# Two chained transformer blocks in fp32: another order of loads, splits and down products in the second block's feed-forwards, and two edits in the first feed-forward

## The chip, the cores and the metric

One core of a Trainium2 chip runs the whole program. The metric is the device time of one execution in microseconds, the median of three runs: 1930.71 us before the change (1929.75 to 1932.2). A difference of 0.2% is 3.9 us.

## What is computed

256 tokens of width 1024 go through a first block of two layers (feed-forward, mixer, feed-forward, each with a layer norm) and a second one of two layers (mixer, feed-forward, gated side input). Cut to what the change touches:

```python
def _swiglu(x, w1, w3, w2):                    # block 1, D_FF = 2816, four times
    return (jax.nn.silu(x @ w1) * (x @ w3)) @ w2

for i in range(DEPTH):                         # block 2, D_FF_2 = 4096, twice
    ...
    u = jax.nn.relu(rms_norm(h, ff_norm[i]) @ w_ff1[i])
    h = h + (u * u) @ w_ff2[i]
```

All of it is fp32 and must be as exact as fp32.

## The kernel before, in words

**Splitting.** TensorE multiplies in a rounded fp32 form. Each matrix is therefore split in a high part (a rounding copy by ScalarE) and a low part (the original less the high part, by VectorE), and a product is three matmuls: high by high, high by low, low by high. A weight unit has 128x2048 values. SyncE loads it into one of four slots of `raw`, ScalarE writes `whi` (for the trace `w_high`), VectorE writes `wlo` (`w_low`), and TensorE uses both in 12 matmuls of 512 columns for one half of the tokens, 24 for both. The slots form a ring. ScalarE may write a slot's high part only when TensorE has used what stood there before, which it learns from the semaphore `unit_used` (helper `used(name)`).

**Pairs (a Strassen-like form with seven products).** Most of the hidden width is computed in groups of four quarter matrices R11, R21, R12, R22 of the weights, loaded into `buf_v`, `buf_q`, `buf_u` and `buf_val`. Seven block products of 12 matmuls give what eight would: `b11`, `b21`, `v`, `x`, `w`, `y`, `b22`. Their weight operands are R11, R21, sums that VectorE forms in place in `buf_v` (`add_to`, one after another: R11+R12 for `v`, then +R22 for `x`, then +R21 for `y`), and R12+R22 in `buf_u` for `w`, which GpSimd makes by a DMA that adds (`w_sum`). The token operands are quarters of x and four sums of them (`form`). Results gather in four banks of `aux` (PSUM); ScalarE copies bank 1 out three times between products (`term1`, `term2`, `term3`) and a last time through the activation (`silu1`); VectorE combines them. The hidden values are then transposed on TensorE (`quad_T(q, 0)`, `quad_T(q, 1)`), split to `yT_high` and `yT_low`, and multiplied by the down weights (`down`, 24 matmuls, one unit of `w_ff2`).

**Block 2's feed-forward** (`ffn2`, `FFN2_ORDER`, `FFN2_DONE`) has two plain groups `h0`, `h1` (transposed by `plain_T(0)` and `plain_T(1)` into banks 2 and 3), whose down units are `d0_0`, `d0_1`, `d1_0`, `d1_1`, and three pairs q = 0, 1, 2, with down units `e0_0` to `e2_3`. Down units fill the time between the block products: pair 0 gets those of the plain groups, pair q those of pair q-1. On TensorE the order before is `d0_0`, `d0_1`, `plain_T(1)`, then for pair 0 `b11 b21 v x (d1_0 first half) w (d1_0 second half) y b22 (d1_1 first half) quad_T(0,0) (d1_1 second half) quad_T(0,1)`.

Product `v` writes bank 3 and must wait till that bank has been read after both `plain_T`, by VectorE's `plain_low_T(1)`:

```python
pe.wait_ge(aux_read[3], aux0[3] + PLAIN2 + q + 1)
block_product(ffn2_unit(i, f"v_{q}"), 3, *form(f, 0), True)
```

**What sets the order.** Each engine has its own list of instructions, written out by hand, and takes them strictly in that order; semaphores hold it where it must wait. SyncE's list of loads is `ffn2` and `quad_load2` there; R11 of the next pair is loaded when `y`'s low part has been made from the same buffer.

**Block 1's feed-forward** (`ffn1`) has the same parts with one down unit and other fills. In the very first one (l = 0, which = 0) GpSimd first adds the negated high part of `b21` to its low part by a DMA (`sums_by_dma`), and then makes `w`'s sum for pair 0 by the second DMA.

Of the kernel before, what the change touches and what calls it, by code (L numbers as in the profile page):

```python
# [121 lines left out]
def ffn2_units():  # L122

    order = ["h0_0", "h0_1", "h1_0", "h1_1", "d0_0", "d0_1",
             "b11_0", "b21_0", "v_0", "x_0", "d1_0", "w_0", "y_0", "b22_0", "d1_1"]
    done = ["h0_0", "h1_0", "d0_0", "d0_1",
            "b11_0", "b21_0", "v_0", "x_0", "w_0", "d1_0", "y_0", "b22_0", "d1_1"]
    for q in range(1, QUADS2):
        e = [f"e{q - 1}_{k}" for k in range(4)]
        order += [f"b11_{q}", f"b21_{q}", f"v_{q}", f"x_{q}", e[0], f"w_{q}", e[1], f"y_{q}", e[2], f"b22_{q}", e[3]]  # L130
        done += [f"b11_{q}", f"b21_{q}", f"v_{q}", f"x_{q}", e[0], f"w_{q}", e[1], f"y_{q}", e[2], f"b22_{q}", e[3]]
# [139 lines left out]
def build(nc, a, out, stop=None):  # L271
    ctx = ExitStack()
    with ctx:
# [100 lines left out]
        w_sum = sem("w_sum")  # L374
        b21_neg = sem("b21_neg")
# [169 lines left out]
        def _(sp):  # L545
# [154 lines left out]
            def ffn2(i):  # L700
# [43 lines left out]
        def _(pool):  # L744
# [42 lines left out]
            def sums_by_dma(l, which):  # L787
# [7 lines left out]
                for q in range(QUADS):  # L795
# [108 lines left out]
        def _(pe):  # L904
# [105 lines left out]
            def ffn2(i, tile1, before_last):  # L1010
# [89 lines left out]
                down("d0_1")  # L1100
                plain_T(1)
                for q in range(QUADS2):
# [22 lines left out]
                    if q > 0:  # L1125
                        down(fill[2])
                    pe.wait_ge(quad_read, combined + 2)
                    block_product(ffn2_unit(i, f"b22_{q}"), 3, *form(f, 3), False)
                    late = "d1_1" if q == 0 else fill[3]
                    down_part(late, 0)  # L1130
                    quad_T(q, 0)
                    down_part(late, 1).then_inc(unit_used, 1)
# [818 lines left out]
        def _(act):  # L1951
# [38 lines left out]
            def ffn2(i, tile1, before_last):  # L1990
# [69 lines left out]
                used("d0_1")  # L2060
                summed(0, 2)
                high_sum("x", 0, R11)
                for q in range(QUADS2):
# [7 lines left out]
                    high_plain("d1_0" if q == 0 else fill[0])  # L2071
                    used(f"b21_{q}")
                    act.wait_ge(w_sum, 16 * quads2_before(i, q) + 16)
                    high_sum("w", q, R12)
                    if q > 0:
                        used(f"v_{q}")
                        high_plain(fill[1])
                    used(f"x_{q}")
                    nc.scalar.copy(term2, aux[:, 1, :]).then_inc(quad_act, 1)
                    summed(q, 3)  # L2080
                    high_sum("y", q, R11)
                    if q > 0:
                        used(fill[0])
                        high_plain(fill[2])
# [4 lines left out]
                    used("d1_0" if q == 0 else fill[1])  # L2089
                    high_plain("d1_1" if q == 0 else fill[3])  # L2090
                    used(f"y_{q}")
                    nc.scalar.activation(silu1, aux[:, 1, :], ACT.Relu).then_inc(quad_act, 1)
                    if q + 1 < QUADS2:
                        loaded(q + 1, R11)
                        high_sum("b11", q + 1, R11)
                        if q > 0:
                            used(fill[2])
                        loaded(q + 1, R21)
                        high_sum("b21", q + 1, R21)
# [3 lines left out]
                        quad_high_T(q, 0)  # L2103
                        quad_high_T(q, 1)
                        used("d1_1" if q == 0 else fill[3])
                        summed(q + 1, 2)
# [1740 lines left out]
```

## Time and profile before

| | before |
|---|---|
| median of 3 runs | 1930.71 us (1929.75 to 1932.2) |
| the profiled execution | 1929.22 us, span 1927.4 us, mean clock share 0.996 |
| TensorE matmul busy | 1881.1 us (98%) |
| VectorE busy | 1494.9 us (78%) |
| ScalarE busy | 1050.0 us (54%) |
| GpSimd busy | 118.9 us (6%) |
| HBM read | 351.39 MB, 183 GB/s over the span |

The profiled execution's time is 1.8 us longer than its span. Matmuls overlap: one of 512 columns is shown with 389 ns, but the next begins 227 ns after it. In a row of the timeline the first number is the start, the second the time to the last end of the row; instructions of VectorE and ScalarE overlap their successor by 0.1 us, so that the starts, not the ends, tell the pace.

### The profile page before, as it was taken

Reading aid. Unit: us, or ns where it says so; the run is one execution under the profiler, and the core shown is the slowest. Engines: PE = TensorE matmul, PEld = TensorE weight load, DVE = VectorE, ACT = ScalarE, POOL = GpSimd, SP = SyncE. Lnnn points to the kernel's source line nnn. Section 1 sums busy time; section 2 is a strip of 40 time slices with the busy share of each in tenths; the row PEclk is TensorE's granted clock in tenths of the full one; section 3 lists DMA queues with packets and bytes.
Section 4 is the critical chain, followed back from the end, with each engine's and each line's share of the span. In section 5 each row is a group of like instructions: output and inputs, shape, how many; then the busy total and the mean of one; then the engine's idle time right before and its main releaser. Section 6 shows DMA issues by size and latency. Waiting matters only on the chain.

```text
span 1927.4 us, 22719 instructions
## 1 busy us (share of the span) xinstructions
PE 1881.1 (98%) x8944; PEld 1538.9 (80%) x8944; DVE 1494.9 (78%) x1663; ACT 1050.0 (54%) x1239; POOL 118.9 (6%) x186
## 2 busy tenths in 40 slices
PE   8999999999999999999999999999999999999999
PEld 7788788887888788878888788787778887777787
DVE  6887766778887888777667888778798766779975
ACT  6555444555555555543564655567655555655553
POOL 2001100001000000110000000011000000100000
PEclk9999999999999999999999999999999999999999
DMA  9865554348764766564445766444385545338651
GB/s 337 266 218 168 203 191 173 141 167 284 240 218 152 241 220 222 185 239 174 142 164 185 252 219 220 151 162 157 130 299 177 197 161 178 121 116 309 181 205 57
DMA packets 179177, 376.99 MB, mean 196 GB/s; under 512 B 7568, under 2 KB 51520, under 8 KB 176256
## 3 DMA queue, kind: packets, MB, share of 16 engines
q1 hardware_dynamic: 170512, 334.85, 49.1%
q0 software_dynamic: 8560, 40.69, 8.7%
q8 instruction: 72, 1.18, 0.2%
q14 instruction: 33, 0.27, 0.0%
HBM read 351.39 MB, written 1.05 MB: 183 GB/s over the span
## 4 chain that ended last, share of the span: by engine, by line
PE 80%; DVE 11%; DMA 3%; ACT 3%; DVEq 1%; issue 1%; SPq 0%; ACTq 0%; POOLq 0%
PE acc L926 49%; PE aux L996 15%; PE aux L926 10%; DVE w_low L2710 3%; DVE w_low L2835 2%; PE aux L941 1%; DMA buf_v<-w_ff 1%; DMA w_raw<-ffn_w 1%; DVE buf_v L2840 1%; PE aux L1364 1%; DVEq L2762 1%; DVE xT_low L2716 1%; DMA buf_u<-buf_val 1%; DMA w_low<-buf_q 1%; PE aux L1211 1%
## 5 line engine op out<-in xcount | busy, mean ns | idle before, releaser
L2710 DVE TENSOR_TENSOR w_low<-w_raw,w_high 128x2048 fp32r<-128x2048 f32 (+1 forms) x246 | 554.1, 2265 | 116.4 <-ACT w_high L1959 113.3
L1959 ACT CAST w_high<-w_raw 128x2048 fp32r<-128x2048 f32 (+1 forms) x246 | 462.2, 1895 | 177.4 <-PE acc L926 155.0
L926 PE MATMUL acc<-w_high,yT_high 128*128 128x512 f32 (+1 forms) x836 | 331.6, 397 | 2.5 <-DVE yT_low L2974 2.0
L926 PE MATMUL acc<-w_high,yT_low 128*128 128x512 f32 (+1 forms) x836 | 325.6, 389 | 0.0
L926 PE MATMUL acc<-w_low,yT_high 128*128 128x512 f32 (+1 forms) x836 | 324.9, 389 | 0.0
L926 PE MATMUL acc<-w_high,xT_high 128*128 128x512 f32 (+2 forms) x752 | 297.9, 396 | 6.9 <-DVE xT_low L2716 4.1
L926 PE MATMUL acc<-w_high,xT_low 128*128 128x512 f32 (+2 forms) x752 | 291.3, 387 | 0.0
L926 PE MATMUL acc<-w_low,xT_high 128*128 128x512 f32 (+2 forms) x752 | 290.9, 387 | 0.0
L926 PEld LDWEIGHTS acc<-w_high,yT_high 128*128 128x128 f32 x836 | 157.0, 188 | 38.2 <-issue 6.6
L926 PEld LDWEIGHTS acc<-w_high,yT_low 128*128 128x128 f32 x836 | 156.9, 188 | 33.0
L926 PEld LDWEIGHTS acc<-w_low,yT_high 128*128 128x128 f32 x836 | 157.2, 188 | 30.0
L926 PEld LDWEIGHTS acc<-w_high,xT_high 128*128 128x128 f32 x752 | 141.6, 188 | 41.4 <-DVE xT_low L2716 5.2
L926 PEld LDWEIGHTS acc<-w_high,xT_low 128*128 128x128 f32 x752 | 141.4, 188 | 28.9
L926 PEld LDWEIGHTS acc<-w_low,xT_high 128*128 128x128 f32 x752 | 141.7, 188 | 26.1
L2141 ACT CAST w_high<-buf_v 128x2048 fp32r<-128x2048 f32 x48 | 91.8, 1913 | 124.8 <-DVE buf_v L2964 81.8
L926 PE MATMUL aux<-w_high,xT_high 128*128 128x512 f32 x384 | 153.6, 400 | 2.6 <-DVE w_low L2710 1.6
L2959 DVE TENSOR_TENSOR w_low<-buf_v,w_high 128x2048 fp32r<-128x2048 f32 x48 | 109.9, 2290 | 52.4 <-ACT w_high L2141 52.4
L926 PE MATMUL aux<-w_high,xT_low 128*128 128x512 f32 x384 | 150.0, 391 | 0.0
L926 PE MATMUL aux<-w_low,xT_high 128*128 128x512 f32 x384 | 149.6, 390 | 0.0
L996 PE MATMUL aux<-w_high,form_high 128*128 128x512 f32 x288 | 113.7, 395 | 7.8 <-DVE w_low L2959 3.9
L996 PE MATMUL aux<-w_low,form_high 128*128 128x512 f32 x288 | 112.6, 391 | 0.0
L996 PE MATMUL aux<-w_high,form_low 128*128 128x512 f32 x288 | 112.6, 391 | 0.0
(411 smaller groups left out, 2754.5 us busy)
## 6 DMA issues: line engine op xcount, KB each, us to landing
w_raw<-w_in SPq DMA_DIRECT2D x52, 1024.0 KB
w_raw<-ffn_w SPq DMA_DIRECT2D x44, 1024.0 KB
w_raw<-w_ff SPq DMA_DIRECT2D x40, 1024.0 KB
w_raw<-ffn_w SPq DMA_DIRECT2D x78, 512.0 KB
buf_u<-buf_val POOLq DMA_DIRECT2D x18, 1024.0 KB, 7.0
w_raw<-w_branch SPq DMA_DIRECT2D x16, 1024.0 KB
buf_q<-ffn_w SPq DMA_DIRECT2D x12, 1024.0 KB, 6.6
buf_v<-ffn_w SPq DMA_DIRECT2D x12, 1024.0 KB, 8.5
```

Source lines behind the costliest of these rows:

```text
L926: last = nc.tensor.matmul(dst, lhs[:, kt, tok], rhs(j), start=(kt == k_first and q == 0), stop=(kt == k_last and q == 2))
L941: last = nc.tensor.transpose(aux[:, b, k * P:(k + 1) * P], src[:, t, kt * P:(kt + 1) * P], ident[:])
L996: last = nc.tensor.matmul(aux[:, b, :], lhs(k), rhs[:, s, k * NC:(k + 1) * NC], start=(first and k == 0 and m == 0), stop=(k == 3 and m == 2),
L1211: last = nc.tensor.transpose(aux[:, b, (2 * f + t) * P:(2 * f + t + 1) * P], h[:, f0:f0 + P], ident[:])
L1364: last = nc.tensor.transpose(aux[0:width, b, (2 * k + t) * P:(2 * k + t + 1) * P], src(t, h), ident[:])
L1959: nc.scalar.copy(whi[:, s, 0:size], raw[:, s, 0:size]).then_inc(slot_hi[s], 1)
L2141: nc.scalar.copy(whi[:, s, :], sum_raw[r]).then_inc(slot_hi[s], 1)
L2710: V.tensor_tensor(wlo[:, s, 0:size], raw[:, s, 0:size], cast(whi[:, s, 0:size]), ALU.subtract)\
L2716: V.tensor_tensor(dst_l[:, k, tok], src, cast(dst_h[:, k, tok]), ALU.subtract)\
L2762: dve.drain()
L2835: V.tensor_tensor(wlo[:, s, :], sum_raw[r], cast(whi[:, s, :]), ALU.subtract)\
L2959: V.tensor_tensor(wlo[:, s, :], sum_raw[r], cast(whi[:, s, :]), ALU.subtract)\
```

## The change

Block 2's feed-forwards, all three pairs of both:

- TensorE: `d0_1` moves from ahead of `plain_T(1)` to behind `v` of pair 0. The four down units of each pair now stand behind `v`, `x`, `w` and (the last) around the transposes: for pair 0 `v d0_1 x d1_0 w (d1_1 first half) y b22 quad_T(0,0) (d1_1 second half) quad_T(0,1)`, for q > 0 `v e0 x e1 w e2 y b22 quad_T(q,0) e3 quad_T(q,1)`.
- Slots: in pair 0 `w` takes the ring place before `x`, which is the slot that `d0_1` leaves.
- VectorE: `d0_1`'s low part goes behind `v`'s, `x`'s low part ahead of `plain_low_T(1)`; `w`'s ahead of the sum for `y` in pair 0; `d1_1`'s ahead of `y`'s; `b11` of the next pair ahead of the product that makes `silu1`'s operand.
- ScalarE: the high parts in the same manner; `w`'s now waits for `d0_1`'s use, and `b11` of pair 1 stands ahead of the activation `silu1`.
- SyncE: `d1_1` and `e0_1` are loaded earlier, `e0_0` later.

First feed-forward of block 1 alone: `activate(1, 0)` and the high and low parts of the first y stand ahead of `b11`'s, and `w`'s sum for pair 0 is made by VectorE behind `x`'s low part (semaphore `w_first`); GpSimd's adding DMA for that pair falls away, and the counts of `w_sum` move by one.

The core of the diff (left out: the tail of the last pair, the semaphore's declaration, the branch for q > 0 where it repeats):

```diff
@@ ffn2_units
     order = ["h0_0", "h0_1", "h1_0", "h1_1", "d0_0", "d0_1",
-             "b11_0", "b21_0", "v_0", "x_0", "d1_0", "w_0", "y_0", "b22_0", "d1_1"]
+             "b11_0", "b21_0", "v_0", "w_0", "x_0", "d1_0", "y_0", "b22_0", "d1_1"]
@@ sync, ffn2
-                for name in ("d1_0", "e0_0", "e0_1", "d1_1"):
+                for name in ("d1_0", "d1_1", "e0_1"):
                     load_ffn2(i, name)
-                for r in (R21, R12, R11, R22):
+                for r in (R21, R12, R11):
                     quad_load2(i, 1, r)
+                load_ffn2(i, "e0_0")
+                quad_load2(i, 1, R22)
@@ gpsimd, sums_by_dma
-                for q in range(QUADS):
+                for q in range(1 if l == 0 and which == 0 else 0, QUADS):
@@ tensor, ffn2
                 down("d0_0")
-                down("d0_1")
                 plain_T(1)
...
                     block_product(ffn2_unit(i, f"v_{q}"), 3, *form(f, 0), True)
+                    down("d0_1" if q == 0 else fill[0])
                     pe.wait_ge(quad_act, terms + 1)
                     block_product(ffn2_unit(i, f"x_{q}"), 1, *form(f, 2), False)
-                    if q == 0:
-                        down_part("d1_0", 0)
-                    else:
-                        down(fill[0])
+                    down("d1_0" if q == 0 else fill[1])
                     pe.wait_ge(quad_act, terms + 2)
                     block_product(ffn2_unit(i, f"w_{q}"), 1, *form(f, 1), False)
+                    late = "d1_1" if q == 0 else fill[3]
                     if q == 0:
-                        down_part("d1_0", 1).then_inc(unit_used, 1)
+                        down_part(late, 0)
                     else:
-                        down(fill[1])
+                        down(fill[2])
@@ scalar, ffn2
-                used("d0_1")
+                used("b11_0")
                 summed(0, 2)
                 high_sum("x", 0, R11)
@@ scalar, ffn1
+                first = l == 0 and which == 0
+                if first:
+                    activate(1, 0)
+                    plain_high_T(0)
                 used("h1_0")
                 loaded(0, R11)
                 high_sum("b11", 0, R11)
@@ vector, ffn2
                 multiply(1, 1)
-                low_plain("d0_1")
                 add_to(0, R11, R12)
                 low_sum("b21", 0, R21)
+                form_low(f, 0)
                 low_sum("v", 0, R11)
+                low_plain("d0_1")
                 add_to(0, R11, R22)
-                for n in range(FORMS):
+                for n in range(1, FORMS):
                     form_low(f, n)
+                low_sum("x", 0, R11)
                 plain_low_T(1)
@@ vector, ffn1
                     low_sum("x", q, R11)
+                    if first and q == 0:
+                        dve.wait_ge(r_full[R22], 16)
+                        V.tensor_tensor(sum_raw[R12], sum_raw[R12], sum_raw[R22], ALU.add).then_inc(w_first, 1)
                     low_plain(f"d{o - 3}")
                     add_to(q, R11, R21)
```

How the lists stand, with the semaphores each row waits on. VectorE in block 2's first feed-forward, from `b11`'s low part (the first row) to `plain_low_T(1)` (the last), before:

```order
L2835 TENSOR_TENSOR w_low<-buf_v,w_high 128x2048 [waits slot_hi0]
L2844 TENSOR_TENSOR buf_k<-buf_k,aux 128x512 [waits act_done]
L2710 TENSOR_TENSOR w_low<-w_raw,w_high 128x2048 [waits slot_hi3]
L2840 TENSOR_TENSOR buf_v<-buf_v,buf_u 128x2048 [waits r_full2]
L2835 TENSOR_TENSOR w_low<-buf_q,w_high 128x2048 [waits slot_hi1]
L2835 TENSOR_TENSOR w_low<-buf_v,w_high 128x2048 [waits slot_hi2]
L2840 TENSOR_TENSOR buf_v<-buf_v,buf_val 128x2048 [waits r_full3]
L2819 TENSOR_TENSOR form_low<-mix_param,form_high 128x512 [waits form_hi] x4
L2850 TENSOR_TENSOR yT_low<-aux,yT_high 128x512 [waits t_hi] x2
```

and the same stretch now:

```order
L2857 TENSOR_TENSOR w_low<-buf_v,w_high 128x2048 [waits slot_hi0]
L2866 TENSOR_TENSOR buf_k<-buf_k,aux 128x512 [waits act_done]
L2862 TENSOR_TENSOR buf_v<-buf_v,buf_u 128x2048 [waits r_full2]
L2857 TENSOR_TENSOR w_low<-buf_q,w_high 128x2048 [waits slot_hi1]
L2841 TENSOR_TENSOR form_low<-mix_param,form_high 128x512 [waits form_hi]
L2857 TENSOR_TENSOR w_low<-buf_v,w_high 128x2048 [waits slot_hi2]
L2732 TENSOR_TENSOR w_low<-w_raw,w_high 128x2048 [waits slot_hi3]
L2862 TENSOR_TENSOR buf_v<-buf_v,buf_val 128x2048 [waits r_full3]
L2841 TENSOR_TENSOR form_low<-mix_param,form_high 128x512 [waits form_hi] x3
L2857 TENSOR_TENSOR w_low<-buf_v,w_high 128x2048 [waits slot_hi0]
L2872 TENSOR_TENSOR yT_low<-aux,yT_high 128x512 [waits t_hi] x2
```

`d0_1`'s low part (from `w_raw`) moved behind `v`'s, and `x`'s low part, which stood behind `plain_low_T(1)`, now stands ahead of it.

ScalarE in pair 0 of the same feed-forward, from the copy `term1` on, before (`w` is the row from `buf_u`, `silu1` the ACTIVATE, and the row behind it `b11` of pair 1):

```order
L2070 COPY mix_param<-aux 128x512 [waits unit_used,form_lo]
L1959 CAST w_high<-w_raw 128x2048 [waits slot_full0]
L2005 CAST w_high<-buf_u 128x2048 [waits w_sum,unit_used]
L2079 COPY mix_param<-aux 128x512 [waits unit_used]
L2005 CAST w_high<-buf_v 128x2048 [waits sum_done]
L2086 COPY mix_param<-aux 128x512 [waits unit_used]
L2005 CAST w_high<-buf_val 128x2048 [waits r_full3]
L1959 CAST w_high<-w_raw 128x2048 [waits slot_full0,unit_used]
L2092 ACTIVATE mix_param<-aux 128x512 [waits unit_used]
L2005 CAST w_high<-buf_v 128x2048 [waits r_full0]
```

and now:

```order
L2069 COPY mix_param<-aux 128x512 [waits unit_used,form_lo]
L1958 CAST w_high<-w_raw 128x2048 [waits slot_full1,unit_used]
L2004 CAST w_high<-buf_u 128x2048 [waits w_sum,unit_used]
L2087 COPY mix_param<-aux 128x512 [waits unit_used]
L1958 CAST w_high<-w_raw 128x2048 [waits slot_full0]
L2004 CAST w_high<-buf_v 128x2048 [waits sum_done]
L2096 COPY mix_param<-aux 128x512 [waits unit_used]
L2004 CAST w_high<-buf_val 128x2048 [waits r_full3]
L2004 CAST w_high<-buf_v 128x2048 [waits r_full0,unit_used]
L2109 ACTIVATE mix_param<-aux 128x512 [waits unit_used]
```

`b11` of pair 1 (from `buf_v`, waiting on its load `r_full0`) moved ahead of the activation; the `unit_used` of `w` is now that of `d0_1`.

VectorE in the first feed-forward of block 1, from `x`'s low part to `w`'s, before and then now:

```order
L2959 TENSOR_TENSOR w_low<-buf_v,w_high 128x2048 [waits slot_hi1]
L2710 TENSOR_TENSOR w_low<-w_raw,w_high 128x2048 [waits slot_hi0]
L2964 TENSOR_TENSOR buf_v<-buf_v,buf_q 128x2048 [waits r_full1]
L2959 TENSOR_TENSOR w_low<-buf_u,w_high 128x2048 [waits slot_hi3]
...
L2999 TENSOR_TENSOR w_low<-buf_v,w_high 128x2048 [waits slot_hi1]
L3074 TENSOR_TENSOR buf_u<-buf_u,buf_val 128x2048 [waits r_full3]
L2732 TENSOR_TENSOR w_low<-w_raw,w_high 128x2048 [waits slot_hi0]
L3004 TENSOR_TENSOR buf_v<-buf_v,buf_q 128x2048 [waits r_full1]
L2999 TENSOR_TENSOR w_low<-buf_u,w_high 128x2048 [waits slot_hi3]
```

One more addition of a whole unit stands between `x`'s low part and that of the down unit `d1`.

## Rows read from the trace of the kernel before

**Rows 1.** The page: span, and busy time of TensorE and VectorE (share, instructions).

```profile
span 1927.4 us, 22719 instructions
PE 1881.1 (98%) x8944; PEld 1538.9 (80%) x8944; DVE 1494.9 (78%) x1663; ACT 1050.0 (54%) x1239; POOL 118.9 (6%) x186
```

**Rows 2.** Waits of TensorE: who waited for whom, us in total, times, longest.

```profile
PE aux L1058 <- DVE mix_param L2863: 4.7, 2, 3.0
...
PE aux L996 <- DVE w_low L2959: 3.9, 1, 3.9
PE aux L996 <- DVE yT_low L2850: 3.5, 4, 1.7
...
PE acc L926 <- DVE yT_low L2974: 2.0, 1, 2.0
```

**Rows 3.** Chain of waits in order of time (start, us, what): TensorE's paces.

```profile
60.38 4.51 PE aux L996 x12
...
1448.42 13.24 PE aux L996 x48
1461.66 5.44 PE acc L926 x24
...
1786.03 11.18 PE aux L996 x48
```

**Rows 4.** Busy time by stretch: us, engines' busy time, granted clock (PEclk), DMA share, GB/s.

```profile
60.40:63.50 3.10, 3.10 (x7) 2.44 (x8) 3.10 (x2) 1.59 (x1) 0.00 (x0) 0.50 0.68 198
1445.60:1452.70 7.10, 5.89 (x18) 4.63 (x19) 6.76 (x6) 2.62 (x3) 0.00 (x0) 0.53 0.45 92
1783.20:1789.00 5.80, 4.06 (x21) 3.33 (x22) 5.80 (x5) 1.21 (x3) 0.00 (x0) 1.00 0.63 132
```

**Rows 5.** Timeline of block 2's first feed-forward, TensorE: start of `d0_0`, `v`, `quad_T(0,1)`.

```profile
1398.32 0.39 PE L926 MATMUL acc<-w_high,yT_high 128*128 128x512 f32 x1
...
1416.19 0.50 PE L996 MATMUL aux<-w_high,form_high 128*128 128x512 f32 x1 [0.30 <-DVE yT_low L2850]
...
1445.62 1.60 PE L1058 MATMUL aux<-ident,mix_param 128*128 128x128 f32 x8 [3.03 <-DVE mix_param L2863]
```

**Rows 6.** Timeline, VectorE: `b11` low, forms, `plain_low_T(1)`; last, layer 2's `b11` low.

```profile
1398.62 2.29 DVE L2835 TENSOR_TENSOR w_low<-buf_v,w_high 128x2048 fp32r<-128x2048 f32 x1 [1.39 <-ACT w_high L2005]
1400.83 0.68 DVE L2844 TENSOR_TENSOR buf_k<-buf_k,aux 128x512 f32<-128x512 f32 x1
...
1412.43 2.50 DVE L2819 TENSOR_TENSOR form_low<-mix_param,form_high 128x512 fp32r<-128x512 f32 x4
1414.84 1.29 DVE L2850 TENSOR_TENSOR yT_low<-aux,yT_high 128x512 fp32r<-128x512 f32 x2
...
1737.61 2.29 DVE L2835 TENSOR_TENSOR w_low<-buf_v,w_high 128x2048 fp32r<-128x2048 f32 x1 [1.34 <-ACT w_high L2005]
```

**Rows 7.** Timeline, ScalarE: pair 1's `b11` high part, behind its load.

```profile
1435.59 1.91 ACT L2005 CAST w_high<-buf_v 128x2048 fp32r<-128x2048 f32 x1 [1.43 <-DMA buf_v<-w_ff]
```

**Rows 8.** Chain of waits, the loads of R11: pair 0, then pair 1.

```profile
1391.09 5.51 DMA buf_v<-w_ff
...
1427.76 7.81 DMA buf_v<-w_ff
```

**Rows 9.** Timeline of the first feed-forward, VectorE: low parts of `b11`, `x`, `d1`, `w`.

```profile
33.56 2.29 DVE L2959 TENSOR_TENSOR w_low<-buf_v,w_high 128x2048 fp32r<-128x2048 f32 x1 [2.07 <-ACT w_high L2141]
...
47.44 2.29 DVE L2959 TENSOR_TENSOR w_low<-buf_v,w_high 128x2048 fp32r<-128x2048 f32 x1 [0.18 <-ACT w_high L2141]
50.31 2.29 DVE L2710 TENSOR_TENSOR w_low<-w_raw,w_high 128x2048 fp32r<-128x2048 f32 x1 [0.58 <-ACT w_high L1959]
...
57.94 2.29 DVE L2959 TENSOR_TENSOR w_low<-buf_u,w_high 128x2048 fp32r<-128x2048 f32 x1 [3.13 <-ACT w_high L2141]
```

**Rows 10.** Chain of waits there: GpSimd's two adding DMAs.

```profile
32.04 11.18 DMA w_low<-buf_q
...
43.88 12.05 DMA buf_u<-buf_val
```

More of the change, by code:

```diff
@@ L2088, in ffn2 @@
                     high_sum("b22", q, R22)
[L2089 to L2092, printed above, removed]
                     if q + 1 < QUADS2:
-                        loaded(q + 1, R11)
-                        high_sum("b11", q + 1, R11)
-                        if q > 0:
-                            used(fill[2])
-                        loaded(q + 1, R21)
-                        high_sum("b21", q + 1, R21)
+                        if q == 0:
+                            used("d1_0")
+                            loaded(1, R11)
+                            high_sum("b11", 1, R11)
+                        else:
+                            used(fill[2])
+                            loaded(q + 1, R21)
+                            high_sum("b21", q + 1, R21)
+                        used(f"y_{q}")
+                        nc.scalar.activation(silu1, aux[:, 1, :], ACT.Relu).then_inc(quad_act, 1)
+                        if q == 0:
+                            loaded(1, R21)
+                            high_sum("b21", 1, R21)
+                        else:
+                            loaded(q + 1, R11)
+                            high_sum("b11", q + 1, R11)
+                        quad_high_T(q, 0)
                         used(f"b22_{q}")
@@ L2102, in ffn2 @@
                         high_sum("v", q + 1, R11)
[L2103 removed]
                         quad_high_T(q, 1)
[L2105 to L2107 removed]
                     else:
                         tail = [f"e{q}_{k}" for k in range(4)]
+                        used(f"y_{q}")
+                        nc.scalar.activation(silu1, aux[:, 1, :], ACT.Relu).then_inc(quad_act, 1)
                         high_plain(tail[0])
[L2111 removed]
+                        quad_high_T(q, 0)
                         high_plain(tail[1])
@@ L2186, in ffn1 @@
                 high_sum("b11", 0, R11)
-                activate(1, 0)
-                plain_high_T(0)
+                if not first:
+                    activate(1, 0)
+                    plain_high_T(0)
                 for n in range(FORMS):
@@ L2909, in ffn2 @@
                     V.tensor_tensor(term1, aux[:, 0, :], term1, ALU.add).then_inc(quad_read, 1)
+                    low_plain("d1_1" if q == 0 else fill[2])
                     low_sum("y", q, R11)
@@ L2920, in ffn2 @@
-                    V.tensor_tensor(silu1, silu1, aux[:, 1, :], ALU.mult).then_inc(h_ready, 1)
                     if q + 1 < QUADS2:
-                        low_sum("b11", q + 1, R11)
-                        add_to(q + 1, R11, R12)
-                        low_sum("b21", q + 1, R21)
+                        if q == 0:
+                            low_sum("b11", 1, R11)
+                        else:
+                            low_sum("b21", q + 1, R21)
+                        dve.wait_ge(quad_act, terms + 4)
@@ new lines, in ffn2 @@
+                        V.tensor_tensor(silu1, silu1, aux[:, 1, :], ALU.mult).then_inc(h_ready, 1)
+                        if q == 0:
+                            add_to(1, R11, R12)
+                        dve.wait_ge(unit_used, ffn2_done(i, f"b22_{q}"))
+                        V.tensor_tensor(term2, aux[:, 3, :], term2, ALU.subtract).then_inc(quad_read, 1)
+                        squared_relu(term2, combined + 3)
+                        if q > 0:
+                            low_sum("b11", q + 1, R11)
+                            add_to(q + 1, R11, R12)
@@ L2925, in ffn2 @@
+                        quad_low_T(q, 0)
+                        if q == 0:
+                            low_sum("b21", 1, R21)
+                        low_sum("v", q + 1, R11)
+                        quad_low_T(q, 1)
+                        add_to(q + 1, R11, R22)
                     else:
                         tail = [f"e{q}_{k}" for k in range(4)]
+                        dve.wait_ge(quad_act, terms + 4)
+                        V.tensor_tensor(silu1, silu1, aux[:, 1, :], ALU.mult).then_inc(h_ready, 1)
@@ L3006, in ffn1 @@
                 low_plain("d0")
+                first = l == 0 and which == 0
+                if first:
+                    dve.wait_ge(aux_full[2], n_aux[2].k + 1)
+                    plain_low_T(0)
                 low_sum("b11", 0, R11)
-                dve.wait_ge(aux_full[2], n_aux[2].k + 1)
-                plain_low_T(0)
+                if not first:
+                    dve.wait_ge(aux_full[2], n_aux[2].k + 1)
+                    plain_low_T(0)
                 multiply(1, 0)
```

81 lines of the change are left out of this document (44 added, 37 removed).

## The prediction

> **What bounds the kernel now.** I read the page first: matmuls fill 98% of the span [rows 1], so only TensorE's gaps can be won or made. The view of waits says which gaps: 3.9 us for a low part `w` (the first feed-forward, behind GpSimd's adding DMA), 2.0 us for a low part of y (there too), up to 3.0 us for `mix_param` and 1.7 us for `yT_low` around the transposes of pair 0 in block 2 [rows 2]. The reader is to see that these places are few, and that the other pairs have none. The chain of waits gives the prices: 12 matmuls take 2.72 us when they follow one another (5.44 for 24), but 4.51 right after the 3.9 us gap; 48 take 11.18, but 13.24 after the 3.0 us gap [rows 3]. The view by stretches says why: after those two gaps the granted clock is 0.50 and 0.53, the lower level (1.2 GHz), and after two gaps of 1.7 us it stayed at 1.00 (2.4 GHz) [rows 4]. So a long gap costs itself and about 2 us more (1.79 by the first pair of numbers, 2.06 by the second), short ones only themselves.
>
> **How I work it out.** I take the written lists of the changed kernel and place each instruction behind its predecessor and behind what it waits for, with the paces of the trace: VectorE 2.2 us for a whole unit and 0.6 for a bank (the starts in [rows 6]; a row shown alone has 0.1 more), ScalarE 1.9 us from start to release for a high part [rows 7], TensorE 2.72 us for 12 matmuls and 0.9 for a `quad_T` (estimated from its 8 short matmuls; 1.60 at the low clock [rows 5]). In block 2, times are counted from the start of `b11`'s low part: 1398.62 in layer 1, 1737.61 in layer 2 [rows 6]. Up to there nothing changed.
>
> **Block 2, the wait ahead of `v`.** `v` may start only when VectorE has read bank 3 in `plain_low_T(1)`; the trace shows this very wait (0.30 us), with `v` at 1416.19, that is +17.6 [rows 5]. The change puts more work ahead of that read. VectorE's list in order: `b11` 2.2, multiply 0.6, sum 2.2, `b21` 2.2, one form 0.6, `v` 2.2, `d0_1` 2.2, sum 2.2, so at +14.4; meanwhile three forms 1.8, but `x`'s high part can only begin when the sum is there and takes 1.9 and the handovers, so `x`'s low part starts at +16.5 and ends at +18.7; `plain_low_T(1)` 1.3: bank 3 is free at +20.0 and `v` starts at **+20.1**, 2.5 later. At the same time TensorE arrives earlier, since `d0_1` (5.44) moved behind `v`: `d0_0` starts at 1398.32, or -0.3 [rows 5], then 5.44, `plain_T(1)` 0.8, `b11` and `b21` 5.44, +11.4. It stands for about **8.7 us** with the down unit that could have filled it queued behind the wait. After a gap twice as long as the one that brought the low clock, I charge the low clock once: 2.0 us.
>
> **Block 2, the rest of pair 0.** Let E be the end of `d0_1`: +20.1, plus `v` and `d0_1` 8.2, plus 0.1 to its release, plus 2.0 clock, +30.4. `w`'s high part now waits for E, as it gets the slot of `d0_1`. From E: high 2.0, low 2.2, the sum for `y` 2.2, the combination of `term1` 0.6, low of `d1_1` 2.2, low of `y` 2.2: E+11.4. TensorE has seven groups of 12 meanwhile (`x`, two of `d1_0`, `w`, half of `d1_1`, `y`, `b22`), 19.0 us to E+18.9, and none of them waits. But `y`'s low part is also what lets SyncE load R11 for pair 1, and ScalarE now takes pair 1's `b11` ahead of `silu1`, and VectorE its low part ahead of the product behind it. Issue at E+11.5; a landing took 5.51 us with nothing ahead of it and 7.81 behind two others [rows 8] (in the trace the high part of pair 1's `b11` waited for the second one, but stood behind the activation [rows 7]). I take 5.5, as the two loads ahead are issued earlier now and are through; +17.0. High 1.9, low 2.2, product 0.7, handovers 0.3: `quad_T(0,0)` starts at E+22.1, **3.2 us** after `b22`. It then is followed by 2.72, the second transpose 0.9, and the reads of banks 1 and 0: pair 1's `b11` starts at about E+27.2.
>
> VectorE is behind by then. In order from E+27.0: `b21` 2.2, `v` 2.2, the second transpose's low parts 1.2, the sum 2.2, and `e0_0` 2.2, which TensorE now wants right behind `v`: with handovers E+37.1. TensorE would be there at E+35.5; **1.6 us** more. A low clock after the 3.2 us gap would be paid inside this 1.6, so I charge none. From `e0_0` on I find TensorE behind nothing: each down unit of 5.44 gives VectorE two whole units and more, while a pair has 14 large ones (31 us) in 49 us.
>
> **Sum for block 2.** `e0_0` starts at +30.4+37.1 = +67.5. Before, the same amount of TensorE work was through at the end of pair 1's `v`: `b11` of pair 1 started at 1448.42, +49.8 [rows 3], plus 2.06 of low clock, plus three groups 8.2: +60.0. Layer 1 loses 7.5. In layer 2, pair 1's `b11` started at 1786.03, +48.4, at full clock [rows 3]: +56.6, and it loses **10.9**. Together +18.4. The loads of `d1_1`, `e0_1`, `e0_0` that moved cost nothing: they land long ahead of their use (slots free since `h1` and `d0_1`).
>
> **The first feed-forward.** y's parts first: the first y's low part is made before `b11`'s (33.56 [rows 9]), so TensorE does not wait the 2.0 us of [rows 2]. `b21` is then held by the adding DMA, which lands at 43.2 [rows 10], where TensorE arrives at 43.1: 0.4 lost. VectorE does not get faster: `b11` starts 0.9 later behind the y, the chain to `x` 0.3 later, so that `x`'s low part starts at 47.8 (47.44 before [rows 9]) and ends at 50.0, while TensorE is there at 49.0: 1.2 us gap. `w`'s sum (2.2, in place of the DMA of 12.05 us that landed at 55.9 [rows 10]) follows, `d1`'s low part ends at 54.4, and TensorE is there at 52.9: 1.7. The sum for `y` and `w`'s low part end at 58.9; TensorE is there at 57.3: 1.7. So `w` starts at 58.95 where it did at 60.38, 1.4 earlier. If these three short gaps leave the clock at 1.00, as two of 1.7 us did [rows 4], another 1.8 is saved (2.72 in place of 4.51 [rows 3]): **-3.2**. Behind `w`, VectorE is ahead of TensorE again.
>
> **Total.** -3.2 + 7.5 + 10.9 = +15.2. The profiled execution took 1929.2 (span 1927.4), so 1944.4 for its like; the median shown is 1.5 higher: **1945.9 us**.
>
> On the landing of R11 the Trainium skill, page "DMA: Bandwidth & Descriptors", section "Anatomy of one DMA", has a price: 2.0 us and the bytes over 436 GB/s, which is an estimated 4.4 us for 1 MB. The rows do not bear it out (5.51 at the least), and by it the total would be 2.2 lower, 1943.7.
>
> **Bounds.** R11 lands after 5.5 to 7.8: up to 2.3 more in each layer. The clock: 1.8 to 4 us after the 8.7 us gap (4 if it recovers only after twice as many matmuls, since one stretch at the low level lasted 3.1 us and the other 7.1 [rows 4]), and up to 2 more after the gap of 3.2. First feed-forward: -1.4 to -5. Not all of one sign: **1938 to 1955**.
>
> **Rivals.**
> 1. *The wait ahead of `v` is not the read of `plain_low_T(1)`, so that it ends with `v`'s own low part* (faster). Then `v` starts right behind `b21` at +11.5, E is +19.8, and `e0_0` stands at +56.9 against +60.0 and +56.6: -3.1 and +0.3, with -3.2 a total of -6.0, **1924.7**. It decides if the bank's read count asks for one plain group only. For it: moving `d0_1` back is only sensible so. Against it: the written wait and the 0.30 us row whose releaser is `yT_low` [rows 5]. 10%.
> 2. *Only the work counts*: clock and load cost nothing, `v` waits at +20.1 and then all is packed. 31.8 us to pair 1's `b11`: +51.9 against +51.9 and +48.4; 0 and +3.5, with -3.2 **1931.0**, no change. Against it: both gaps are of the size that brought the low clock. 4%.
> 3. *Both gaps bring the low clock in full and R11 lands late*: +2 and +2.3 in each layer, **1954**, slower still. 16%.
>
> **Chances.** My forecast 70%, within 1940 and 1950. A difference of 0.2% (3.9 us) is what the measurement can tell. Faster 0.10, same 0.04, slower 0.86.
>
> **What would show it.** In the profile after: a gap of about 8 to 9 us on TensorE ahead of `v` in both of block 2's feed-forwards, ended by `yT_low`, with the granted clock at 0.5 behind it; a gap of about 3 us ahead of `quad_T(0,0)`, ended by `mix_param` (the product of `silu1`); one of 1 to 2 us ahead of `e0_0`, ended by a low part from `w_raw`; in the first feed-forward no gap ahead of `d0`, three of 1 to 2 us at `x`, `d1` and `w`. I am wrong if `v` starts right behind `b21`, or if VectorE does not come to `plain_low_T(1)` at +18.7.

## The result, and the profile after

| | before | changed |
|---|---|---|
| median | 1930.23 us (1929.2 to 1932.2, 4 runs) | 1951.95 us (1951.57 to 1953.47, 4 runs) |
| the profiled execution | 1929.22 us, span 1927.4 us | 1953.47 us, span 1951.6 us |
| mean clock share | 0.996 | 0.989 |

The ratio is 1.0113, 95% interval [1.0095, 1.013]: 1.1% slower. The forecast was 1945.9 us (1938 to 1955): right in its sign and range, 6 us too low. The two profiled executions are 24.2 us apart and the medians 21.7, since one of them is 1.0 under its median and the other 1.5 above. From the page of the changed kernel, beside [rows 1]:

```profile
span 1951.6 us, 22714 instructions
PE 1888.0 (97%) x8944; PEld 1544.5 (79%) x8944; DVE 1496.1 (77%) x1664; ACT 1047.3 (54%) x1239; POOL 118.4 (6%) x185
```

The same 8944 matmuls are busy for 6.9 us more, and the rest of the 24.2 us is idle time. The waits of TensorE (who waited for whom, us in total, times, longest), beside [rows 2]:

```profile
PE aux L999 <- DVE yT_low L2872: 18.7, 2, 9.6
PE aux L1061 <- DVE mix_param L2953: 8.5, 2, 4.4
...
PE aux L999 <- ACT mix_param L2240: 4.0, 4, 1.6
PE acc L929 <- DVE w_low L2732: 3.8, 7, 1.4
...
PE aux L999 <- DVE w_low L2999: 1.1, 1, 1.1
```

The first row is the wait ahead of `v` in both of block 2's feed-forwards, the second that ahead of `quad_T(0,0)`; the other three include the short gaps of the first feed-forward (1.56, 1.40 and 1.07 us there).

To see where the time goes I subtract, at marks along the program, the start of the same transposes on TensorE in the trace of before from that in the other (the mark at the end of layer 1's feed-forward starts at 1546.74 before and at 1554.68 after). In us, negative is earlier; the last kernels are those of the experiments:

| mark (start before) | changed | a | b | c | d | e | f | g | h | j | k |
|---|---|---|---|---|---|---|---|---|---|---|---|
| behind the first feed-forward (90.10) | -2.8 | -2.6 | -2.8 | -2.8 | -2.7 | -2.6 | -2.6 | +0.2 | -2.9 | -1.5 | -1.5 |
| behind a layer norm (655.06) | -1.4 | -1.2 | -2.9 | -2.8 | -1.3 | -1.2 | -2.8 | +0.2 | -3.1 | -1.7 | 0.0 |
| behind block 1 (1263.27) | -1.6 | -1.6 | -3.3 | -2.6 | -1.8 | -2.2 | -3.8 | -0.5 | -3.9 | -2.3 | -1.0 |
| end of block 2's first feed-forward (1546.74) | +7.9 | -1.4 | -3.4 | +5.4 | -3.3 | +9.6 | -2.8 | -1.5 | -3.3 | -4.2 | +0.7 |
| end of its second (1882.29) | +24.1 | +1.1 | +0.7 | +17.3 | -1.1 | +22.2 | +2.2 | +1.1 | 0.0 | -0.4 | +6.5 |

(j and k began 1.6 and 1.3 us later in the program's first steps, which all their marks contain.)

In the changed kernel the first feed-forward gives 2.8, block 2's first feed-forward takes 9.5 and its second 16.2. The chain of waits of layer 1 (start, us, what), beside [rows 3, 8]:

```profile
1390.48 10.01 DMA buf_u<-w_ff
...
1416.52 1.21 DVE yT_low L2872 x2
...
1417.77 4.61 PE aux L999 x12
1422.39 5.46 PE acc L929 x24
...
1427.87 1.92 ACT w_high L2004
...
1437.11 2.21 DVE w_low L2857
...
1439.34 6.66 DMA buf_v<-w_ff
...
1446.08 1.91 ACT w_high L2004
...
1448.02 2.29 DVE w_low L2857
1450.31 0.60 DVE mix_param L2953
```

and of layer 2:

```profile
1739.08 10.54 DMA buf_u<-w_ff
...
1766.92 5.49 PE aux L999 x12
1772.40 5.72 PE acc L929 x24
...
1789.62 6.97 DMA buf_v<-w_ff
...
1801.54 1.97 PE aux L1061 x8
1803.51 4.40 PE acc L929 x12
```

The reader is to see the alternation that the prediction laid out: VectorE up to `plain_low_T(1)`, then `v` and `d0_1` on TensorE, then the high part of `w` (which has `d0_1`'s slot), VectorE's list down to `y`'s low part, the load of R11, and `b11`'s two parts ahead of the product. TensorE's gaps in the timeline of layer 1, beside [rows 5], `v`, `quad_T(0,0)`, `e0_0`:

```profile
1417.77 0.80 PE L999 MATMUL aux<-w_high,form_high 128*128 128x512 f32 x1 [9.10 <-DVE yT_low L2872]
...
1450.96 1.09 PE L1061 MATMUL aux<-ident,mix_param 128*128 128x128 f32 x8 [4.09 <-DVE mix_param L2953]
...
1465.69 0.50 PE L929 MATMUL acc<-w_high,yT_high 128*128 128x512 f32 x1 [0.21 <-DVE w_low L2732]
```

And the view by stretches (length, busy us of PE, PEld, DVE, ACT, POOL with counts, granted clock, DMA share, GB/s), beside [rows 4]: the gap ahead of `v`; what follows it in layer 1 and in layer 2; what follows `quad_T(0,0)` in layer 1 and in layer 2:

```profile
1408.60:1417.70 9.10, 0.08 (x1) 0.00 (x0) 8.89 (x9) 4.18 (x3) 0.00 (x0) 0.63 0.68 195
1417.70:1420.70 3.00, 2.93 (x7) 2.35 (x8) 2.22 (x2) 0.00 (x0) 0.00 (x0) 0.50 0.00 0
1766.90:1772.40 5.50, 5.48 (x13) 4.33 (x14) 2.16 (x1) 0.00 (x0) 0.00 (x0) 0.50 0.00 0
1452.00:1456.40 4.40, 4.40 (x15) 3.44 (x14) 4.37 (x6) 2.63 (x3) 0.87 (x1) 0.62 1.01 326
1801.50:1807.90 6.40, 6.36 (x22) 5.37 (x23) 6.37 (x6) 2.97 (x3) 0.86 (x1) 0.58 0.95 305
```

All four places run at or near the lower level of the clock; before, only one of layer 1 did, and none of layer 2.

### The profile page after: what moved, and what is told of

It reads as the page before. It is cut to its first block, busy times and chain, and to the rows that moved or that the text cites. A ratio compares the mean times of both kernels' runs of the same rounds, so it can differ in the third digit from the quotient of the medians.

```text
span 1951.6 us, 22714 instructions
## 1 busy us (share of the span) xinstructions
PE 1888.0 (97%) x8944; PEld 1544.5 (79%) x8944; DVE 1496.1 (77%) x1664; ACT 1047.3 (54%) x1239; POOL 118.4 (6%) x185
## 4 chain that ended last, share of the span: by engine, by line
PE 77%; DVE 13%; ACT 3%; DMA 3%; DVEq 1%; issue 1%; SPq 0%; ACTq 0%
PE acc L929 48%; PE aux L999 13%; PE aux L929 10%; DVE w_low L2732 4%; DVE w_low L2857 2%; DVE buf_v L2862 1%; PE aux L944 1%; DMA buf_u<-w_ff 1%; DMA w_raw<-ffn_w 1%; ACT w_high L2004 1%; ACT w_high L2155 1%; DMA buf_v<-w_ff 1%; ACT w_high L1958 1%; DVE buf_v L3004 1%; PE aux L1363 1%
```

## The experiments

Ten kernels ran, in three groups, each beside runs of the kernel before on the same chip (its medians 1929.78, 1930.35 and 1930.51 us; single runs from 1924.41 to 1934.29). The changed kernel ran only beside the result above, at 1951.95; differences from it below cross those groups, in which the kernel before moved by 0.7 us at most.

**a: the first feed-forward alone.** The kernel before with the `ffn1` parts of the diff and nothing of block 2.

> The kernel before with the two edits of the first feed-forward alone; block 2 as before. My theory (these edits win 3.2 us, all loss is in block 2's new lists): 1927.2, 3 us below the kernel before, three gaps of 1.1 to 1.7 us at x, d1 and w, the clock at 1.00 there, and everything behind the first feed-forward as before. Rival (VectorE's extra unit of 2.2 us is paid back later, or the freed adding DMA changes the loads): no change, 1930.

Measured 1928.55 us (1924.75 to 1931.71, 10 runs), ratio 0.9994 [0.9984, 1.0004]. The 2.6 us stand behind the first feed-forward, as expected, but are not all there at the end: 1.4 go at a layer norm and 2.5 in block 2's second feed-forward, whose code is that of before and whose gaps are the same within 0.2; there and at the layer norm the clock fell, and in the trace of before it did not (last section). So the time is not told apart from before, and what the change loses is all in block 2.

**h and g: its two edits apart.** h has `w`'s sum by VectorE only, g only y's parts first. From a:

```diff
@@ h: scalar and vector, ffn1
-                if first:
-                    activate(1, 0)
-                    plain_high_T(0)
...
@@ g: gpsimd and vector, ffn1
-                for q in range(1 if l == 0 and which == 0 else 0, QUADS):
+                for q in range(QUADS):
...
-                    if first and q == 0:
-                        dve.wait_ge(r_full[R22], 16)
-                        V.tensor_tensor(sum_raw[R12], sum_raw[R12], sum_raw[R22], ALU.add).then_inc(w_first, 1)
```

> The kernel before with w's sum by VectorE in the first feed-forward alone, y's parts where they were. My theory: the 2.0 us gap ahead of d0 stays, w starts at 58.7 instead of 60.38 and at full clock: 3.4 us earlier behind w, as much as both edits give together (2.8 measured there), so that y's order is worth nothing beside it. Rival (the two edits add up): 1 us or less.

> The kernel before with y's high and low part ahead of b11's in the first feed-forward of block 1, W by GpSimd's adding DMA as before. My theory: the 2.0 us gap ahead of d0 goes, but b21 (low part by GpSimd's adding DMA) and w are still held by DMAs that land at the same time, so b21 waits up to 2 us more and behind w the same transposes of TensorE stand within 0.3 us of before: time within 0.1% of before. Rival (y's order is worth its own 2.0 us): 2 us earlier behind w, ratio 0.999.

Measured: h 1929.17 us (1926.6 to 1931.3, 10 runs), 0.9995 [0.9985, 1.0004]; g 1930.67 us (1928.69 to 1933.03, 11 runs), 1.0003 [0.9994, 1.0011]. The timeline of TensorE in h, then in g, each gap up to `w`:

```profile
36.78 0.47 PE L927 MATMUL acc<-w_high,yT_high 128*128 128x512 f32 x1 [2.03 <-DVE yT_low L2979]
...
58.97 0.50 PE L997 MATMUL aux<-w_high,form_high 128*128 128x512 f32 x1 [0.80 <-ACT mix_param L2223]
```

```profile
50.07 0.47 PE L997 MATMUL aux<-w_high,form_high 128*128 128x512 f32 x1 [1.15 <-DVE w_low L2965]
...
59.35 0.76 PE L997 MATMUL aux<-w_high,form_high 128*128 128x512 f32 x1 [3.55 <-DVE w_low L2965]
```

With VectorE's sum alone `w` starts at 58.97, as with both edits (59.00), and TensorE is 2.9 us earlier behind it (58.7 and 3.4 were expected). y first alone takes the 2.0 us gap away; 1.15 come back at `x`, and `w` starts 1.0 earlier than before. That 1.0 goes in the clock: from `w`'s start the next two groups of 12 begin after 5.3 and 3.1 us, where it was 4.3 and 2.7 before, so that the mark stands at +0.2. The clock behind like gaps differs from one execution to another (last section), so g alone does not show that y's order is worth nothing; that it adds nothing beside `w`'s sum is shown by h against both edits, and by j. The whole gain of this part is the adding DMA that fell away.

**b: VectorE reads bank 3 directly behind `v`'s low part.**

```diff
                 low_sum("v", 0, R11)
+                plain_low_T(1)
                 low_plain("d0_1")
...
                 low_sum("x", 0, R11)
-                plain_low_T(1)
```

> The changed kernel with one line moved: VectorE's plain_low_T(1) stands directly behind v's low part, ahead of d0_1, the second sum, three forms and x. My theory (v waits for this read of bank 3, with a down unit queued behind it): the gap ahead of v (9.1 and 9.6 us) goes, d0_1 ends 10.3 us earlier in layer 1 and 11.6 in layer 2, the gap ahead of quad_T(0,0) stays at 3 to 4.5; 1952 less 22, 1930. Rival (VectorE is the limit of the stretch in any order, so that the gap only moves to x or w): at most 5 us less, 1947 to 1952.

Measured 1930.78 us (1929.58 to 1932.77, 10 runs), ratio 1.0008 [0.9999, 1.0018], 21.2 us faster than the changed kernel. Its waits of TensorE from 1725 to 1830 us (layer 2):

```profile
PE aux L1061 <- DVE mix_param L2953: 4.4, 1, 4.4
PE aux L999 <- DVE yT_low L2872: 0.4, 1, 0.4
...
```

and the stretch in which the changed kernel stood:

```profile
1408.60:1417.70 9.10, 8.78 (x39) 6.96 (x38) 8.87 (x7) 6.02 (x4) 0.00 (x0) 1.00 0.52 153
```

The place of one read of 1.2 us on VectorE carries nearly the whole loss. By the marks, block 2 takes 22 us less than in the changed kernel: the gaps of 9.10 and 9.59, and most of the 1.9 and 3.1 that the clock took behind them. The gap ahead of `quad_T(0,0)` stays, 4.41, as expected, and yet b is not told apart from before, which had gaps of its own there.

**e: `x`'s low part behind `plain_low_T(1)`, nothing else.** It is the one instruction that stands ahead of the read now and did not before (the others only changed places), and it waits for ScalarE.

```diff
-                low_sum("x", 0, R11)
                 plain_low_T(1)
+                low_sum("x", 0, R11)
```

> The changed kernel with VectorE's x low part behind plain_low_T(1) again, nothing else. My theory: v starts 2.5 us earlier in both layers, and all of it stays to the end of the pair, since d0_1 (whose use the chain of w, y and R11 waits for) ends 2.5 us earlier: 1947. Rival (x's low part is the next wait, so that nothing is won): 1952.

Measured 1949.71 us (1947.52 to 1951.59, 4 runs), ratio 1.0103 [1.0088, 1.0118]. TensorE's timeline in layer 1:

```profile
1416.28 0.80 PE L999 MATMUL aux<-w_high,form_high 128*128 128x512 f32 x1 [7.14 <-DVE yT_low L2872]
...
1452.33 1.97 PE L1061 MATMUL aux<-ident,mix_param 128*128 128x128 f32 x8 [5.66 <-DVE mix_param L2953]
```

The first gap is 2.0 shorter in layer 1 (and 3.0 in layer 2, 6.6 us), but the second is 1.6 and 0.9 longer. That is the landing of R11, which took 8.24 and 7.87 us here and 6.66 and 6.97 in the changed kernel. In layer 1 the clock took more, too: `v` and `d0_1` took 11.4 us instead of 10.1. So by the marks layer 1 took 2.2 us more than in the changed kernel and layer 2 3.5 less. The time lies halfway between the expected 1947 and the rival's 1952, and neither held; what the place of `x`'s low part alone is worth stays open.

**k: `d0_1` ahead of `v` on TensorE**, all else as changed (and the list of `unit_used` counts to match):

```diff
+                    if q == 0:
+                        down("d0_1")
                     pe.wait_ge(aux_read[3], aux0[3] + PLAIN2 + q + 1)
                     block_product(ffn2_unit(i, f"v_{q}"), 3, *form(f, 0), True)
-                    down("d0_1" if q == 0 else fill[0])
+                    if q > 0:
+                        down(fill[0])
```

> The changed kernel with one swap on TensorE: d0_1 stands ahead of v instead of behind it (and the count of unit_used with it); VectorE's and ScalarE's lists are untouched, so bank 3 is free no sooner. My theory (the price is that a down unit that could run is queued behind the wait): v starts where it did, with a gap of 2 to 3 us in place of 9 behind d0_1 and one of 1.5 ahead of it, at full clock; the stretch to e0_0 is 9 to 10 us shorter in each layer: 1932. Rival (the late read of bank 3 is the whole price, whatever stands around it): at most the clock is saved, 2 us in a layer, 1948.

Measured 1932.98 us (1930.25 to 1935.83, 10 runs), ratio 1.0013 [1.0004, 1.0023]. TensorE's waits from 1380 to 1475 us:

```profile
PE acc L929 <- DVE w_low L2735: 3.0, 2, 1.7
PE aux L999 <- DVE yT_low L2875: 2.0, 1, 2.0
PE aux L1061 <- DVE mix_param L2956: 1.3, 1, 1.3
...
```

VectorE's late read is still there, but the gap ahead of `v` is 2.0 and the one ahead of `d0_1` 1.65 (the other 1.4 of the first row stand ahead of `e0_0`): 3.6 in place of 9.1, less by the 5.4 us of the unit that is no longer queued behind the wait. Since `d0_1` is used earlier, `w` gets its slot earlier, and R11 lands 5.63 us after its issue instead of 6.66: the gap at `quad_T(0,0)` shrinks to 1.3. The full clock was expected and did not come (last section). k is 19.0 us faster than the changed kernel and still slower than before, by less than 0.2%.

This and b show one mechanism from its two sides: the loss needs both the late read and the unit behind the wait. In numbers, of the gap of 9.1 the 5.4 of `d0_1` are work that TensorE did ahead of `v` before, 3.1 are the read, which comes 20.7 us behind `b11`'s low part instead of 17.6, and 0.3 was there before. e and k together, which would undo both, were not run.

**c: the activation and its product ahead of pair 1's `b11`** (ScalarE and VectorE; there `b11`'s low part goes behind the product and the squares, and the sum behind the transposed low parts):

```diff
@@ scalar, ffn2
-                        if q == 0:
-                            used("d1_0")
-                            loaded(1, R11)
-                            high_sum("b11", 1, R11)
...
                         used(f"y_{q}")
                         nc.scalar.activation(silu1, aux[:, 1, :], ACT.Relu).then_inc(quad_act, 1)
...
+                        loaded(q + 1, R11)
+                        high_sum("b11", q + 1, R11)
```

> The changed kernel with ScalarE's silu1 and VectorE's two products and squares for the transposes ahead of pair 1's b11 (pair 0 only). My theory (the second gap, 4.1 and 4.4 us ahead of quad_T(0,0), is the landing of R11 in a queue ahead of silu1): no gap ahead of quad_T(0,0), but gaps of 1 to 2 us at pair 1's first products, since R11 lands no sooner; 1.5 to 2 us less in each layer plus a low clock of 1 to 2.7 us that stays away: 1946, between 1944 and 1949. Rival (b22 or term2 come late): the gap stays at 3 to 4 us, 1952.

Measured 1947.41 us (1946.62 to 1948.99, 4 runs), ratio 1.0098 [1.0083, 1.0113]. Its timeline in layer 1: `v`, then `b21`, `v` and `e0_0` of the next pair:

```profile
1416.72 0.80 PE L999 MATMUL aux<-w_high,form_high 128*128 128x512 f32 x1 [9.04 <-DVE yT_low L2869]
...
1455.48 0.47 PE L999 MATMUL aux<-w_high,xT_high 128*128 128x512 f32 x1 [2.08 <-DVE w_low L2854]
1458.79 0.50 PE L999 MATMUL aux<-w_high,form_high 128*128 128x512 f32 x1 [0.34 <-DVE yT_low L2869]
1463.19 0.50 PE L929 MATMUL acc<-w_high,yT_high 128*128 128x512 f32 x1 [1.35 <-DVE w_low L2729]
```

The gap of 4.1 at `quad_T(0,0)` is gone and 3.8 us of shorter gaps stand in its place, all ended by low parts: VectorE is late either way. What the edit wins is 4.5 us over both layers (1946 expected), and the clock stays up behind gaps of this size here.

**d: b and c together.**

> Both moves of the two kernels above on the changed kernel. My theory: 1930 less 6, 1924, faster than both kernels, with no gap over 3 us in block 2's pairs. Rival (the two gaps cover one another's work): 1928 to 1932, no gain over the kernel with the first move alone.

Measured 1927.81 us (1925.82 to 1930.14, 10 runs), ratio 0.9994 [0.9985, 1.0003]. b took 21.2 off the changed kernel, c 4.5, both 24.1, so they nearly add; no gap of block 2 is over 3 us, as expected, but 1924 was not reached, since the short gaps of c stay, and the rival's 1928 is the nearer number.

**f: three more moves on top of d**, meant to close them: `b21` of pair 1 ahead of its `b11`, the second transpose's parts ahead of `v`'s, `e0_0`'s low part ahead of the third sum (ScalarE's high parts to match).

```diff
@@ vector, ffn2, pair 0
                         V.tensor_tensor(silu1, silu1, aux[:, 1, :], ALU.mult).then_inc(h_ready, 1)
+                        if q == 0:
+                            low_sum("b21", 1, R21)
...
-                            low_sum("b21", 1, R21)
+                            quad_low_T(0, 1)
                         low_sum("v", q + 1, R11)
+                        if q == 0:
+                            low_plain("e0_0")
```

> The kernel with both moves (y behind v, silu1 ahead of b11), and in pair 0 also b21 of pair 1 right behind the product of silu1, the second transpose's low parts ahead of v's, and e0_0's ahead of the third sum. My theory (VectorE's list decides the 2.1 and 1.4 us gaps at pair 1's b21 and e0_0): e0_0 starts 1.4 us earlier in each layer, 1925, faster than before by 0.2 to 0.3%. Rival (the gap only moves from b21 to b11): 1928, nothing won.

Measured 1933.75 us (1931.56 to 1937.06, 9 runs), ratio 1.0019 [1.0009, 1.0029]: worse. In layer 1 the gaps moved: to `b11` (1.71 us) and `v` (1.41), from `e0_0` to `e0_1` (1.34), and a new one of 1.69 stands ahead of `b22` of pair 1. Neither number was right.

**j: d without y first.**

> The changed kernel with VectorE reading bank 3 directly behind v's low part, the activation and the products ahead of pair 1's b11 (both edits of d_both), and without y's parts first in block 1's first feed-forward; of that, only W by VectorE stays. My theory: the first feed-forward keeps its 2.9 us (b11, v and x are not held by y's parts), and block 2 stays as in d_both, so that the time is that of d_both within 0.1%: ratio to before 0.9985 to 1.000. Rival (y first carries part of d_both's time): 1.5 to 2 us slower than d_both, ratio 1.0005 or more.

Measured 1927.84 us (1926.21 to 1930.82, 12 runs), ratio 0.999 [0.9981, 0.9998], with d's median. It is the best version found: 0.1% under before by its interval, which is less than the 0.2% taken as a difference here. So no version is shown to beat before by an amount that counts.

## Why the prediction was right, and where it was off

**The wait ahead of `v`: right.** VectorE starts its read at 1416.4 and `v` at 1417.77, 20.7 us behind `b11`'s low part (20.1 forecast; 21.4 in layer 2), after a gap of 9.10 and 9.59 (8.7 forecast). b and k show the cause from both sides. Rival 1 (the wait ends with `v`'s own low part) is refuted by the releaser and by b. What is missing in the step is a load: the sum for `v` now stands 2.2 us earlier in VectorE's list, at +2.8, and R12, 10.01 and 10.54 us under way, landed behind that time. VectorE waited 0.54 and 1.21 us for it; that is the +0.6 and +1.3. The trace of before had this: R12's load, issued at 1392.06, landed at +3.4 in layer 1 and at +4.0 in layer 2, hidden by the sum's old place at +5.0 (view of the tile, 1391 to 1406 us, before):

```profile
L697 SPq DMA_DIRECT2D buf_u<-w_ff x1: 500/500/500, 1392.1 to 1392.1; - x1
...
DMA to landing us min/median/max: 10.0/10.0/10.0
```

**The chain from E to `quad_T(0,0)`: right in its links, one too short.** The order (`w` by `d0_1`'s slot, the sum, `d1_1`, `y`, the load, `b11`, the product) is what the chain shows. From E (1427.85) to the transposes (1450.96) it took 23.1 us, in layer 2 23.4, against 22.1. The link is the landing of R11, put at 5.5 us since the two loads ahead of it would be "through": it took 6.66 and 6.97. They were not through. R21's and R12's were issued 4.6 to 5.0 us ahead of R11's, and R12's landed 3.8 us (layer 2: 3.1) behind R11's issue. In k, where R12's was issued over 7 us ahead and landed within 0.6 us of R11's issue, R11 took 5.63 and 5.52. The bound, 7.8, covered it. The price in the Trainium skill, page "DMA: Bandwidth & Descriptors", section "Anatomy of one DMA", by which 1 MB takes an estimated 4.4 us, is 2.3 to 2.6 too low here; the section gives it for DMAs that GpSimd issues, and these are issued by SyncE.

**The clock: charged once, it fell twice.** Behind the gap ahead of `v` 12 matmuls took 4.61 us in layer 1 (2.72 at full speed: 1.9, against 2.0) and 5.49 in layer 2 (2.8, and 0.3 in the unit behind). Behind the gap ahead of `quad_T(0,0)` it fell too, which the prediction held to be "paid inside this 1.6" of waiting ahead of `e0_0`. In layer 1 that is what the rows show: the half unit behind the transposes took 4.59 from start to last end instead of about 3.0, and the gap ahead of `e0_0` was 0.21 instead of 1.6. In layer 2 the transposes (1.97 for 1.03) and that unit (4.75) cost 2.7 together, more than the wait could hide, and no gap was left.

**Behind `e0_0`: "I find TensorE behind nothing" was wrong.** Low parts were late again, by 0.45 us in layer 1 and by 0.67 and 0.43 in layer 2. That is not pair 0's lateness carried on: VectorE stood idle in pair 1 for 4.33 us (5.39 in layer 2), since ScalarE waited for the load of `e0_3`, which SyncE's list has behind R12's and R12's behind `w`'s low part. In layer 2 this load makes the 0.67, which stands ahead of `b22` of pair 1 (chain of waits: start, us, what):

```profile
1825.61 8.53 DMA w_raw<-w_ff
...
1834.21 1.92 ACT w_high L1958
...
1842.12 3.00 PE aux L999 x12
```

The 0.45 and 0.43 stand ahead of `e1_0`, the place that the prediction worked out for pair 0 only. From the end of `b22` (1493.36) TensorE has 15.4 us of work to it, and VectorE's chain, the reading of bank 3, the squares, `b11`, sum, ScalarE's `v`, `v`, the second transpose, sum, `e1_0`, takes 15.8. A gap costs more than it shows: where 0.45 is shown, the next group starts 3.33 us behind the last instead of 2.72, and the one behind it 2.85. With that the stretch behind `e0_0` took 1.0 and 1.7 us more than before.

Added up, block 2 lost 25.7 us against 18.4:

| step | layer 1 | layer 2 |
|---|---|---|
| forecast loss | 7.5 | 10.9 |
| R12 landing ahead of `v` | +0.6 | +1.3 |
| `v` and `d0_1` (clock) | -0.2 | +0.9 |
| E to `quad_T(0,0)`: R11 | +1.0 | +1.3 |
| `quad_T(0,0)` to `e0_0` | -0.3 | +0.3 |
| the same mark in before, read 0.1 too early | -0.2 | -0.1 |
| behind `e0_0` | +1.0 | +1.7 |
| measured | 9.5 | 16.2 |

(Each row is rounded by itself, so that the columns add up within 0.1; each compares times from the mark that the prediction counts from.) With +0.4 in the first feed-forward, +1.5 at the layer norm and -0.3 from there to the end of block 1, this makes of the forecast 15.2 the measured 24.1.

So the mechanism held, and the sum was too small in three places, all of one sign: late loads (4.2), the stretch behind `e0_0`, put at nothing (2.7), and the clock (0.7). The median, 1951.95, lies inside the bounds but outside the 1940 to 1950 to which the forecast gave its 70%. Rival 3 named two of them, the second low clock and the late load, and its 1954 is nearer to the result than the forecast; at 16% it was held too unlikely. Rival 2 (only the work counts, 1931) has the gap ahead of `v` too; it fell with the clock behind it (1.9 and 3.1 us) and with the second gap (4.09 and 4.39).

**The first feed-forward: right.** `w` starts at 59.00 (58.95 forecast), with gaps of 1.07, 1.40 and 1.56 us (1.2, 1.7, 1.7) and the clock at 1.00 in the stretch ahead of it:

```profile
54.40:59.00 4.60, 2.97 (x12) 2.17 (x12) 4.60 (x3) 2.43 (x3) 0.00 (x0) 1.00 0.70 228
```

The gain was 2.8 for 3.2. One releaser was another: `w` waited for ScalarE's copy (`mix_param`, L2240), not for its own low part. The copy stands behind the high part of block product `y` in ScalarE's list, and that one waited for VectorE's sum (2.45 us, to 56.57); h, without the first y's parts ahead, has the same releaser. And half of the part, y's order, adds nothing to the other (h). What was not foreseen is that 1.5 of it did not last to block 2.

## What to carry to other kernels

Where an engine takes its list strictly in order, never queue work that can run behind a wait whose releaser you have just moved later: one read of 1.2 us behind 8.7 us of other work on VectorE, with a 5.4 us unit behind the wait on TensorE, made a gap of 9 us per layer, and moving either of the two (b, k) won back 21 and 19 of the 22 us. When a step moves earlier in a list, look again at each load that it needs: R12's, hidden by the old place, had been 10 us under way in the trace of before already. And when two waits alternate between the same two engines, closing one shows the next (c, f), so compute the whole alternation ahead of placing anything.

## What was not expected of the hardware

The same gap did or did not bring the low clock. At a layer norm TensorE stands for 2.29 us, and resumes at 636.00 in the changed kernel and at 636.05 in b, whose code is the same up to there. Behind it the granted clock was 0.57 in the changed kernel (first row) and 1.00 in b (second):

```profile
637.00:640.00 3.00, 3.00 (x12) 2.31 (x11) 0.69 (x1) 0.59 (x1) 1.13 (x2) 0.57 1.05 400
```

```profile
637.00:640.00 3.00, 3.00 (x17) 2.47 (x16) 1.38 (x2) 1.77 (x3) 1.16 (x2) 1.00 1.06 401
```

The marks show the 1.5 us in the changed kernel and in a, d, e and k, and not in b, c, f, g, h and j. In a, block 2's second feed-forward has gaps of 1.83 and 1.71 us, where before has 1.66 and 1.71 and [rows 4] shows 1.00; in the same stretch the clock was 0.50:

```profile
1783.20:1789.00 5.80, 4.23 (x10) 3.37 (x11) 5.51 (x6) 1.94 (x3) 0.00 (x0) 0.50 0.35 71
```

A gap of 1.99 us brought it in k (0.59 in the 3 us behind it), one of 2.08 in c did not. So the prediction's reading that short gaps cost only themselves holds for one execution, not for all. What decides was not tried. It may be why the runs of one kernel spread by 7 us, in which gains of 2 to 3 us drown: a's fastest, 1924.75 us, has a mean clock share of 0.997, its slowest, 1931.71, one of 0.993.

In layer 1 of the changed kernel the clock fell only when the work had been resumed: the stretch behind the gap of 4.09 us starts at 0.97 and is at 0.62 from 1452 us on, so that the price of the gap fell on matmuls behind the transposes.

```profile
1450.80:1452.00 1.20, 1.04 (x9) 1.04 (x10) 1.20 (x2) 0.34 (x1) 0.00 (x0) 0.97 1.03 410
```

Loads of 1 MB that SyncE issued together landed one behind the other. The four of pair 0 in the changed kernel, R11, R21, R12 and R22, were issued within 1.5 us and landed 5.5, 7.8, 10.0 and 12.2 us after their issue in layer 1, and 5.4, 8.4, 10.5 and 12.7 in layer 2. What such a load takes is thus read from its place among the others.
